# Norm entries begun inside the program that feeds them, in a two-block transformer kernel on one Trainium2 core

## What is computed

```python
# first block, each layer
h = rms_norm(x, attn_norm[l]);  proj = h @ w_in[l]
mix = concatenate([attention A, differential attention B, gated scan C])
x = x + mix @ w_out[l]
hf = rms_norm(x, ffn_norm[l]) @ w_up[l]
x = x + (gelu(conv(gate)) * val) @ w_down[l]
# second block, each layer
proj = x @ w_in[l]
mix = rms_norm per head of four mixers
h = layer_norm(ALPHA * x + mix @ w_out[l], ln1_g[l], ln1_b[l])
x = layer_norm(ALPHA * h + peer_ffn(h, ...), ln2_g[l], ln2_b[l])
```

## Time and profile before

| | |
|---|---|
| median of 3 runs | 2827.97 us (2822.35 to 2829.43) |
| the profiled execution | 2826.24 us, its span 2824.5 us |
| TensorE busy | 2651.6 us, 94% of the span |
| VectorE busy | 2054.0 us, 73% |
| ScalarE busy | 1496.3 us, 53% |
| GpSimd busy | 176.2 us, 6% |
| mean granted TensorE clock | 0.979 of full speed |

### The profile page before, as it was taken

One profiled execution on the slowest core, in us unless ns is written; L12 is line 12 of the kernel. 1 busy time (PEld: TensorE's weight loads), 2 busy tenths in 40 slices (PEclk: granted clock), 3 DMA queues, 4 the chain that ended last, 5 costly groups with the idle time before them and its releaser, 6 DMA issues. The chain is left out here.

```text
span 2824.5 us, 56598 instructions
## 1 busy us (share of the span) xinstructions
PE 2651.6 (94%) x17272; PEld 2387.2 (85%) x17272; DVE 2054.0 (73%) x4610; ACT 1496.3 (53%) x2949; POOL 176.2 (6%) x136
## 2 busy tenths in 40 slices
PE   7989999989988899799999999988998999999997
PEld 6869988779977899799988888777998999888886
DVE  5767767767767668877767777787589777677777
ACT  5545556645555444466655555555454566555554
POOL 0000000000000044300000000000344000000000
PEclk9989999989999999999999999999999999999999
DMA  5225654236653477555567777625576555677775
GB/s 194 86 68 166 186 154 162 74 112 184 186 162 101 150 222 225 165 171 176 174 199 233 234 233 232 213 92 174 174 230 192 160 175 171 187 233 235 232 234 179
DMA packets 194306, 503.49 MB, mean 178 GB/s; under 512 B 22561, under 2 KB 88353, under 8 KB 192801
## 3 DMA queue, kind: packets, MB, share of 16 engines
q1 hardware_dynamic: 194208, 502.28, 56.8%
HBM read 467.59 MB, written 34.60 MB: 178 GB/s over the span
## 5 line engine op out<-in xcount | busy, mean ns | idle before, releaser
L182 DVE TENSOR_TENSOR w_lo<-w_raw,w_hi 128x512 fp32r<-128x512 f32 (+1 forms) x1464 | 994.8, 684 | 357.3 <-ACT w_hi L173 337.4
L173 ACT ACTIVATE w_hi<-w_raw 128x512 fp32r<-128x512 f32 (+2 forms) x1592 | 925.7, 621 | 203.4 <-PE banks_right L217 136.7
L215 PE MATMUL up_up<-hT_hi,w_hi 128*128 128x256 f32 x2048 | 595.8, 291 | 26.6 <-DVE w_lo L182 20.5
L217 PE MATMUL up_up<-hT_hi,w_lo 128*128 128x256 f32 x2048 | 582.6, 284 | 0.0
L216 PE MATMUL up_up<-hT_lo,w_hi 128*128 128x256 f32 x2048 | 582.3, 284 | 0.0
L215 PEld LDWEIGHTS up_up<-hT_hi,w_hi 128*128 128x128 f32 x2048 | 396.1, 193 | 31.2 <-DVE w_lo L182 23.9
L227 PE MATMUL banks_left<-w_hi,expert_hi 128*128 128x512 f32 x1024 | 408.1, 399 | 7.8 <-DVE w_lo L182 7.8
L228 PE MATMUL banks_left<-w_lo,expert_hi 128*128 128x512 f32 x1024 | 407.6, 398 | 0.0
L229 PE MATMUL banks_left<-w_hi,expert_lo 128*128 128x512 f32 x1024 | 407.4, 398 | 0.0
L216 PEld LDWEIGHTS up_up<-hT_lo,w_hi 128*128 128x128 f32 x2048 | 395.6, 193 | 0.0
L217 PEld LDWEIGHTS up_up<-hT_hi,w_lo 128*128 128x128 f32 x2048 | 395.0, 193 | 0.0
(11 more groups left out here) (374 smaller groups left out, 3863.6 us busy)
## 6 DMA issues: line engine op xcount, KB each, us to landing
w_raw<-in_peer_u_c SPq DMA_DIRECT2D x256, 512.0 KB, 3.5
w_raw<-in_peer_v SPq DMA_DIRECT2D x256, 512.0 KB, 3.6
w_raw<-in_w_up_c SPq DMA_DIRECT2D x88, 512.0 KB, 3.7
expert_gelu_held<-expert_gelu SPq DMA_DIRECT2D x256, 128.0 KB, 1.7
expert_back<-expert_gelu_held SPq DMA_DIRECT2D x256, 128.0 KB, 3.3
w_raw<-in_w_down SPq DMA_DIRECT2D x44, 512.0 KB, 4.1
w_raw<-in_w_in_r SPq DMA_DIRECT2D x40, 512.0 KB, 3.6
w_raw<-in_w_in_c SPq DMA_DIRECT2D x32, 512.0 KB, 4.0
```

The source lines that it names most:

```text
L173: self.nc.scalar.activation(self.w_hi[:, k % SLOTS, 0:width], self.raw_half(k, width), ACT.Copy).then_inc(self.sem("w_hi_done"), 1)
L182: self.nc.vector.tensor_tensor(self.w_lo[:, k % SLOTS, 0:width], self.raw_half(k, width), self.w_hi[:, k % SLOTS, 0:width].bitcast(F32), A ...
L215: self.nc.tensor.matmul(bank, hi, self.hT_hi[:, c, :], start=(c == 0), stop=False)
L217: last = self.nc.tensor.matmul(bank, lo, self.hT_hi[:, c, :], start=False, stop=(c == DC - 1))
```

## The change

It touches all nine joints and the programs that feed them.

- The last halves of a feeding program go through `last_halves`: first all products of token tile 0, then all of tile 1. In `SecondMiddle` and `DownPhase` it takes the last two chunks together (four halves), in `gated_loop` and `FirstMiddle` the last one (two halves). A semaphore `acc_done` tells when a bank of tile 0 is complete; the banks of tile 1 go by `w_used`. In `DownPhase` the products of the last two expert tiles begin only when the activation pair of the last one is ready.
- The entry object is made before the feeding program, and that program calls its `early_vector` and `early_scalar` at its end: three of the four half adds (0,0), (0,1), (1,0), the first two `w_hi`, and, for RMS, the squares of tile 0 by halves, for layer norm the statistics, root and inverse of tile 0 and of half (1,0). A root is taken of a constant ahead, which brings the activation table in.
- RMS: tile 0 is still turned and scaled by the diagonal; tile 1 is scaled as rows, one half on ScalarE, one on VectorE, and turned by the plain identity (transposes). Epsilon and the first half's mean square go into the root's bias (`base`).
- Layer norm: no centring and no diagonal. Rows become x * r - mean * r in place (ScalarE all of tile 0 and half of tile 1, VectorE the other half), and both tiles are turned by the identity.
- The first four low weight parts are no longer made together: in RMS two stand before the `hT_lo` parts and two between them, in layer norm one before the shifts and three between, in turn4 two before.
- `finish`: ScalarE normalizes tile 0, GpSimd multiplies by gain and adds bias by halves; VectorE does tile 1; four transfers of 256 KB in place of two of 512 KB.
- More semaphores: the last program clears 47 in place of 36.

The core of the diff:

```diff
+    def last_halves(self, pe, chunks, acc, done):
+        for t in range(TT):
+            cols = slice(t * P, (t + 1) * P)
+            for i, (k, act_hi, act_lo) in enumerate(chunks):
+                end = i == len(chunks) - 1
+                for h in range(2):
+                    if t == 0:
+                        pe.wait_ge(self.sem("w_lo_done"), k + h + 1)
+                    hi, lo = self.w_hi[:, (k + h) % SLOTS, :], self.w_lo[:, (k + h) % SLOTS, :]
+                    bank = acc[:, t, h, :]
+                    self.nc.tensor.matmul(bank, act_hi[:, cols], hi, start=False, stop=False)
+                    self.nc.tensor.matmul(bank, act_hi[:, cols], lo, start=False, stop=False)
+                    last = self.nc.tensor.matmul(bank, act_lo[:, cols], hi, start=False, stop=end)
+                    if t == TT - 1:
+                        last.then_inc(self.sem("w_used"), 1)
+                    elif end:
+                        last.then_inc(done, 1)
...
+    def arrived(self, dve, t, h):
+        if t == 0:
+            dve.wait_ge(self.acc_done, h + 1)
+        else:
+            dve.wait_ge(self.K.sem("w_used"), self.k0 - 1 + h)
+    def add_half(self, t, h):
+        x = self.x[:, t, h]
+        return self.K.nc.vector.tensor_tensor(x, x, self.add[:, t, h], ALU.add)
+    def early_vector(self, dve):
+        for t, h in ((0, 0), (0, 1), (1, 0)):
+            self.arrived(dve, t, h)
+            self.add_half(t, h).then_inc(self.added, 1)
+    def early_scalar(self, act, junk=None):
+        for h in range(2):
+            self.K.split_hi(act, self.k0 + h, self.width)
...
+    def vector(self, dve):
+        self.add_half(1, 1).then_inc(self.added, 1)
+        for h in range(2):
+            self.low_weights(dve, h)
+        for j in range(DC // 2):
+            if j in (1, 2):
+                self.low_weights(dve, j + 1)
+            dve.wait_ge(self.hi_done, 2 * j + 2)
+            two = slice(2 * j, 2 * j + 2)
+            self.K.nc.vector.tensor_tensor(self.K.hT_lo[:, two, :], self.ps[:, two, :],
+                                           self.K.hT_hi[:, two, :].bitcast(F32), ALU.subtract).then_inc(self.lo_done, 2)
...
+    def sqrt(self, act, t):
+        act.wait_ge(self.squared, 2 * t + 2)
+        act.wait_ge(self.based, t + 1)
+        ns = self.K.ns[:, t]
+        self.K.nc.scalar.activation(ns[:, 3:4], ns[:, 1:2], ACT.Sqrt, scale=1.0 / D, bias=ns[:, 2:3]).then_inc(self.root, 1)
...
+    def tensor(self, pe):
+        pe.wait_ge(self.scaled, 1)
+        for c in range(DC):
+            self.K.nc.tensor.matmul(self.ps[:, c, 0:P], self.K.x[:, 0, c * P:(c + 1) * P], self.diag[:], start=True, stop=True)
+        for c in range(DC):
+            if c == 0:
+                pe.wait_ge(self.left_half, 1)
+            if c == DC // 2:
+                pe.wait_ge(self.right_half, 1)
+            self.turn(c, 1, self.rows)
...
+        self.sqrt(act, 0)
+        for h in range(2):
+            self.square(act, 1, h, self.spare[:, 0, h])
+        self.sqrt(act, 1)
+        act.wait_ge(self.scaled, 2)
+        A.activation(self.spare[:, 1, 0], self.x[:, 1, 0], ACT.Copy, scale=K.ns[:, 1, 4:5]).then_inc(self.left_half, 1)
+        K.split_hi(act, self.k0 + 2)
+        for j in range(DC // 2):
+            act.wait_ge(self.turned, j + 1)
+            for c in (2 * j, 2 * j + 1):
+                A.activation(K.hT_hi[:, c, :], self.ps[:, c, :], ACT.Copy, scale=self.gain[:, c:c + 1]).then_inc(self.hi_done, 1)
+            if j == 1:
+                K.split_hi(act, self.k0 + 3)
...
+        self.base(dve, 0)
+        if self.add is not None:
+            self.add_half(1, 1).then_inc(self.added, 1)
+        dve.wait_ge(self.root, 1)
+        link(V.reciprocal(K.ns[:, 0, 4:5], K.ns[:, 0, 3:4]))
+        V.tensor_scalar(self.diag[:], K.ident[:], K.ns[:, 0, 4:5], None, ALU.mult).then_inc(self.scaled, 1)
+        self.base(dve, 1)
+        self.low_weights(dve, 0)
+        dve.wait_ge(self.root, 2)
+        V.reciprocal(K.ns[:, 1, 4:5], K.ns[:, 1, 3:4]).then_inc(self.scaled, 1)
+        dve.wait_ge(self.scaled, 2)
+        V.tensor_scalar(self.spare[:, 1, 1], self.x[:, 1, 1], K.ns[:, 1, 4:5], None, ALU.mult).then_inc(self.right_half, 1)
+        self.low_weights(dve, 1)
+        for j in range(DC // 2):
+            if j >= 2:
+                self.low_weights(dve, j)
+            dve.wait_ge(self.hi_done, 2 * j + 2)
+            for c in (2 * j, 2 * j + 1):
+                V.scalar_tensor_tensor(K.hT_lo[:, c, :], self.ps[:, c, :], self.gain[:, c:c + 1],
+                                       K.hT_hi[:, c, :].bitcast(F32), ALU.mult, ALU.subtract).then_inc(self.lo_done, 1)
...
+    def early_vector(self, dve):
+        link = lambda ins: self.K.dve.link(dve, ins)
+        for h in range(2):
+            self.arrived(dve, 0, h)
+            link(self.add_half(0, h))
+            ins = self.stats(0, h)
+        link(ins)
+        self.variance(dve, 0)
+        self.arrived(dve, 1, 0)
+        link(self.add_half(1, 0))
+        self.K.dve.mark(self.stats(1, 0))
+        self.inverse(dve, 0)
+    def early_scalar(self, act, junk=None):
+        if self.gain is not None:
+            super().early_scalar(act)
+        self.K.nc.scalar.activation(self.K.ns[:, 0, 5:6], self.K.eps[:, 1:2], ACT.Sqrt)
+        self.sqrt(act, 0)
+    def last_stats(self, dve):
+        link = lambda ins: self.K.dve.link(dve, ins)
+        link(self.add_half(1, 1))
+        link(self.stats(1, 1))
+        self.variance(dve, 1)
...
+        self.norm_act(act, 0, slice(0, D))
+        self.sqrt(act, 1)
+        self.norm_act(act, 1, slice(0, D // 2))
...
+        self.last_stats(dve)
+        self.inverse(dve, 1)
+        dve.wait_ge(self.ready, 2)
+        V.tensor_scalar(self.x[:, 1, 1], self.x[:, 1, 1], K.ns[:, 1, 3:4], K.ns[:, 1, 4:5], ALU.mult,
+                        ALU.add).then_inc(self.rows_dve, 1)
...
+        self.low_weights(dve, 0)
+        shift(1)
+        low(0, 1)
+        low(1, 1)
+        self.low_weights(dve, 1)
+        low(2, 2)
+        shift(3)
+        self.low_weights(dve, 2)
+        low(4, 2)
+        self.low_weights(dve, 3)
+        low(6, 2)
...
-            down_tile(LAST, 0, at(LAST))
+            pe.wait_ge(lo_done, LAST + 1)
+            K.last_halves(pe, [(at(LAST), ac_hi[:, LAST % 2, :], ac_lo[:, LAST % 2, :])], acc, following.acc_done)
...
+        last = isinstance(n, int) and n == self.ROUNDS - 1 and j >= BODY - 2
+        if last:
+            if j == BODY - 1:
+                first = self.k0 + 2 * SLOTS * n
+                pe.wait_ge(self.lo_done, NK)
+                self.K.last_halves(pe, [(first + 2 * i, self.hi[:, i % 2, :], self.lo[:, i % 2, :]) for i in (BODY - 2, BODY - 1)],
+                                   self.acc, self.following.acc_done)
+            return
...
+            @block.gpsimd
+            def _(pool):
+                pool.wait_ge(norm.rows_act, 1)
+                pool.wait_ge(*rows_in)
+                for h in range(2):
+                    nc.gpsimd.tensor_tensor(x[:, 0, h], x[:, 0, h], gain[:, h], ALU.mult).then_inc(scaled, 1)
+                    pool.wait_ge(scaled, h + 1)
+                    nc.gpsimd.tensor_tensor(x[:, 0, h], x[:, 0, h], bias[:, h], ALU.add).then_inc(by_pool, 1)
...
+                for h in range(2):
+                    K.dve.mark(V.scalar_tensor_tensor(x[:, 1, h], x[:, 1, h], ns[:, 1, 0:1], gain[:, h], ALU.subtract, ALU.mult))
+                dve.wait_ge(norm.root, 2)
+                K.dve.link(dve, V.reciprocal(ns[:, 1, 3:4], ns[:, 1, 2:3]))
+                for h in range(2):
+                    V.scalar_tensor_tensor(x[:, 1, h], x[:, 1, h], ns[:, 1, 3:4], bias[:, h], ALU.mult,
+                                           ALU.add).then_inc(by_dve, 1)
```

413 lines of the change are left out of this document (199 added, 214 removed).

## The result

Four runs of the changed kernel gave 2784.85 to 2789.61 us, median 2786.52; before 2827.55 in the same comparison. The ratio is 0.9859, 95% interval 0.9842 to 0.9876. The forecast was 2812.0 and its range ended at 2803: right in sign, 25 us short, outside the range.

The account below looks back on a forecast made before the run. TensorE, busy 94% of the span, was taken to lose time at the joints. Gains less costs gave 19.7 us at full clock, less 3.7 for the clock: 16.0 us, a median of 2812.0 us, range 2803 to 2823.

Parts of the forecast that it names:

- What is paid: Costs: expert phase waits -2.7 us, more clears and slower products in `finish`, early work in feeding programs nothing.
- RMS joints: norm2 and norm1: earlier first products, tile ends 2.85 us sooner at norm2; gain 5.5 for both norm2, 3.3 norm1.
- rival 1: Clock holds: no half-clock stretch at RMS joints, none over a projection; gain 20 to 21 us, 2807.5; chance 0.2.
- Layer norm joints: ln1, ln2: first projected product at 7.3 us, ln1 tile end 13.0; gains 5.7 for both ln1, 4.0 for ln2.
- The clock term: Half clock at joints costs 0.9 us at each of three layer norm, 0.3 at each of three RMS; 3.7 in all.
- The first tile is VectorE's to pace: At the joints VectorE sets the first projected tile's end, so half clock costs only some 0.6 us there.
- the price of ln2: First product at 7.3 us, eight row chunks of 1.12 and 0.8 waiting end at 17.1; gain 4.0 us.
- rival 2: Identity turns leave the clock low over turns and first tile of six joints; gain 8.5 us, 2819.5; chance 0.2.
- The idle time as a sign of the clock: TensorE idle times from 2.47 us up had a half-clock stretch; those from 1.53 to 1.97 had none of their own.
- turn4: Adds and turns begin at 0.4 us, first product at 3.15 against 5.34; gain 2.2 us.
- expert tiles: Last two tiles of each expert phase wait for the last one's `expert_lo`, 1.25 us plus 0.1, twice; -2.7 us.
- finish: Tail from last product to span's end: GpSimd products at 1.30 us each, 13.4 us against 15.1; gain 1.7 us.

Follow-up runs that it names:

- before_pad160: Kernel before with 160 bytes a partition of unused SBUF behind `epsilons`; 2804.23 us (0.9907).
- after_pad: Changed kernel with 32 bytes a partition of unused SBUF behind `epsilons`; 2812.22 us (0.994).
- before_pad: Kernel before with 32 bytes a partition of unused SBUF behind `epsilons`; 2820.32 us (0.9967).
- after_pad128: Changed kernel with 128 bytes a partition of unused SBUF behind `epsilons`; 2811.79 us (0.9938).
- together: Changed kernel with the first four low weight parts made together before the first `hT_lo` or shift; 2779.57 us (0.9822).
- busy: combined with nine and six more identity turns at each of the three layer norm joints; 2778.11 us (0.9832).
- combined: Changed kernel with low parts placed where VectorE stands still, one expert tile's wait for the other's `expert_lo` dropped, no GpSimd in `finish`; 2773.31 us (0.982).
- before_rest: Kernel before with 32 unused bytes behind `epsilons` and 32 more ahead of `expert_hi` and `expert_lo`; 2821.20 us (0.9978).

## Why the prediction was wrong

**The step that failed** is the list in "What is paid". It costed every instruction that the change moves and took the products in between as fixed. The two persistent tiles were in the diff and had no term, nor had any address. The runs put 23.3 us there by the products' pace (before_pad160: 23.8 faster with unused bytes alone). No rival and no bound of the range covered it, which is why the time fell 16 us under the range.

**The change's own worth.** It can now be read with the operands placed alike: changed kernel against before_pad160 17.7 us (both 226.7 ns); after_pad against before_pad 8.1, corrected by the 0.5 ns between their paces 9.6; after_pad128 against before 16.2, less 5.8 for its pace 10.4. In the first of these the feed-forward operands are not alike (232.7 and 229.2 ns, 1.8 us for 528 products). The joints in the two profiles give 11.3. The forecast was 16.0: right in sign, within what these readings span, but above three of the four. By itself the change is worth 0.3 to 0.6%.

**RMS joints: right.** Idle 1.63 (1.6 to 1.7 forecast), next tile 9.83 (9.8), 5.5 us for both norm2 (5.5 forecast), norm1 2.95 (3.3), layer 0's -0.5 (0, down to -0.5). The clock held there, as rival 1 had it, so its 0.3 each wasn't paid. VectorE's part held as well: its evictions and the two low parts between them ran from 4.9 to 9.3 us (4.85 to 9.3 forecast). What the prediction didn't see is that VectorE stands still for 1.04 us just ahead of them, room for those two parts: together shows 0.8 us more to be had.

**Layer norm joints: first product right, the rest too good.** Idle 2.74 and 2.92 (2.7 to 2.8), first products 7.54, 7.63 and 7.29 (7.3). Next tile 14.07 and 13.82, not 13.0. The clock term was mis-sized: half clock lasted until 915.1, 15.8 us behind the last product, not 10.7 to 13.4. "The first tile is VectorE's to pace" failed there: at 0.213 us apart its 24 products take 5.1 us by themselves, and VectorE's last `hT_lo` was ready at 911.77, 1.6 us before the tile's end. From these rows I estimate that half clock cost 0.9 us in the tile (six products at 0.12 behind 911.77 would end at 13.15) and 0.7 behind it (9.37 from the next tile to the 97th product, 8.64 at full clock): 1.6 where 0.9 stood. The two ln1 joints gave 2.5; with 1.6 each for the clock that is the 5.7 of the sum at full clock. ln2 gave 0.6 in place of 4.0 less 0.9. There half clock ran from 1775.3 to 1785.5, over 17 products 0.35 us apart in place of 0.19; VectorE's last `hT_lo`, at 1784.10, would have held a full-clock tile too, so I estimate 1.5 us for the clock. Behind its first tile TensorE then waits for a `w_lo` three times (0.27, 0.27 and 0.28 us), each made between products of 1.22 us of `x` with the norm's rows (L600, L604), the first of which waited for its rows' transfer until 1786.23; the price of ln2 had only one such wait, of 0.8. What is left of its shortfall stays open. By rival 2 the three layer norm joints would have given 4.2; they gave 3.1, but not by its cause. (The six prices for the clock add to 3.6 and not 3.7.)

**Rival 2's cause fell, as far as it was tested.** Identity turns don't lower a full clock: eight of them ran at 1.00 in each norm2 joint, and in busy thirty-one at ln1, 56 products in a window at 1.00. The rule of the Trainium skill (TensorE: Matmul & The Clock Gate, "Part 4: PE-mode transpose") that full clock doesn't engage for transposes was weighed at 0.2; every row here speaks against it where the clock was full when they began. Whether turns lift a low clock as other products do, no run shows: at ln1 of layer 0 the stretch is 13.6 us long with identity turns in it and was 6.8 with the longer turns before.

**The idle time as a sign of the clock** was read too strictly. norm1 of layer 1 idled for 2.82 us in the changed kernel at full clock throughout; in combined it idled for 2.84 and a half-clock stretch lay over its turns (3.52 us for the first sixteen, 2.05 in the changed kernel). These stretches also come and go between kernels that do the same work there: before_pad160 lacks the one at 143.6 of the kernel before, busy has one that combined lacks. What decides it stays open; they are most of the 3 us or so by which kernels differ in stages that no edit touches.

**turn4** 2.1 (2.2 forecast), **expert tiles** -2.3 (-2.7), both right. **finish** 0.5, not 1.7: GpSimd's products took 1.26 to 1.71 us, near the 1.30 that was taken, but VectorE's took 1.33 to 1.75 each beside them, where the sum had none of its time in it. The Trainium skill (SBUF — State Buffer, "SBUF: two separate sides") has an exclusive lock between GpSimd and VectorE instructions with two SBUF inputs. The rows agree for VectorE (two such products in 1.41 us alone, 3.00 and 3.23 beside GpSimd's); what GpSimd's take alone no run shows. The prediction used the rule for GpSimd's end alone and not for VectorE's. The last transfer's issue ended 10.4 us behind the last product (9.4 forecast), and the tail behind it was 4.3 us with 47 clears (4.0 forecast).

## What to carry to other kernels

When a change allocates, frees or resizes a persistent SBUF tile, write down which operands move, and compare the distance from start to start of the same products in both traces before explaining anything else. For a long run of float32r products with 512 moving columns, try the stationary operand at the moving operand's place within 256 bytes; for products with 256 columns try them apart, since there distance 128 was the faster one. And before work is moved into an engine's pauses, find those pauses in the timeline: a part put between evictions that another engine waits for is on the path; two parts put ahead of them, where VectorE stood still for 1.04 us, made norm2's first product 0.4 us later and its tile's end 0.8 sooner.

## What was not expected of the hardware

The distance of consecutive 128x512 float32r products depends on where their two operands start against each other within 256 bytes: 226.7 ns at distance 0 and 232.4 to 234.3 at the five others that were run, with nothing waiting and full clock. Away from 0 the distances repeat in a fixed pattern for hundreds of us (238, 229 in before_pad's second layer; 231, 231, 238 in before_rest's; 238, 237, 231, 234, 235, 234, 231 in the kernel before, a period of seven), at 0 all are 225 to 228. Products of 256 columns go the other way: 852 in 100 us at distance 0 and 859 at 128. The Trainium skill (TensorE: Matmul & The Clock Gate, "Step-by-step: what each phase is for") gives TensorE two independent read ports, so that loading the next weights doesn't take from the running product. These rows show 6 to 8 ns more for each product of 512 columns unless the two operands stand alike; no run here separates the loads from the products' own reading, so whether it is the loads that take it is not shown. Why 256 bytes, why the sign turns with the number of columns, and whether other types show it, stays open.
